# Nine runs of four modulation blocks instead of eighteen runs of two, between the weight products of a fused two-layer kernel

## The reference: what is computed

```python
mod = jax.nn.silu(c) @ w_mod[l] + b_mod[l]
sh_m, sc_m, ga_m, sh_f, sc_f, ga_f = [m[:, None, :] for m in jnp.split(mod, N_MOD, axis=-1)]
mod_c = jax.nn.silu(c_ctx) @ w_mod[l] + b_mod[l]
```

## Time and profile before

| what | value |
|---|---|
| median of 3 runs | 2073.24 us (2072.97 to 2073.39) |
| the profiled execution, own time | 2074.61 us |
| its span, first to last instruction | 2072.8 us |
| TensorE busy | 2036.8 us, 98% of the span |
| weight loads of TensorE busy | 1775.6 us, 86% |
| VectorE busy | 1526.2 us, 74% |
| ScalarE busy | 1036.0 us, 50% |
| moved by DMA | 454.53 MB, mean 219 GB/s |
| mean granted clock of TensorE | 0.996 |

### The profile page before, as it was taken

How to read it: one execution, slowest core, us unless ns; L and a number is a source line. 1 busy time by engine, 2 the same in 40 slices (tenths; PEclk the granted TensorE clock), 3 DMA queues, 4 the chain that set the end, 5 groups by cost and what they waited for, 6 DMA issues and landing times.

```text
span 2072.8 us, 29839 instructions
## 1 busy us (share of the span) xinstructions
PE 2036.8 (98%) x11900; PEld 1775.6 (86%) x11900; DVE 1526.2 (74%) x2369; ACT 1036.0 (50%) x1548; POOL 56.7 (3%) x57
## 2 busy tenths in 40 slices
PE   8999999999999999999999999999999999999998
PEld 8999999878888888898888888878888888888886
DVE  6888886869798786678888896576766756645655
ACT  6876445656423323545555555555445434434543
POOL 0000010110000000000000000200000000000000
PEclk9999999999999999999999999999999999999999
DMA  7778898667534586444447987555875765565553
GB/s 284 241 255 298 299 340 270 240 198 256 167 101 153 207 297 236 149 136 143 132 143 275 374 300 260 182 165 180 292 263 187 254 212 191 190 213 190 191 192 113
DMA packets 124251, 454.53 MB, mean 219 GB/s; under 512 B 14288, under 2 KB 14672, under 8 KB 123472
## 3 DMA queue, kind: packets, MB, share of 16 engines
q1 hardware_dynamic: 124112, 452.62, 64.4%
HBM read 448.35 MB, written 4.22 MB: 218 GB/s over the span
## 4 chain that ended last, share of the span: by engine, by line
PE 72%; DVE 2%; ACT 1%; issue 0%; DVEq 0%; ACTq 0%
PE bank L923 72%; DVE WL L1643 1%; DVE AR L1650 0%; DVE AR L1643 0%; DVE SR L1650 0%; ACT WH L1228 0%; ACT AR L1228 0%; ACT AR L1229 0%; ACT L1229 0%; PE bank L1080 0%; PE bank L1119 0%; ACT SR L1229 0%; DVE WF L1681 0%; DVE AR L1738 0%; DVE AR L2142 0%
## 5 line engine op out<-in xcount | busy, mean ns | idle before, releaser
L923 PE MATMUL bank<-SR,WH 128*128 128x512 f32 (+1 forms) x5216 | 1395.3, 354 | 16.8 <-DVE WL L1643 7.9
L1643 DVE TENSOR_TENSOR WL<-WF,WH 128x1024 fp32r<-128x1024 f32 x636 | 775.7, 1226 | 266.1 <-ACT WH L1228 262.6
L1228 ACT ACTIVATE WH<-WF 128x1024 fp32r<-128x1024 f32 x636 | 671.5, 1057 | 539.7 <-PE bank L923 472.1
L923 PE MATMUL bank<-SR,WL 128*128 128x256 f32 (+1 forms) x3936 | 924.2, 287 | 1.7 <-DVE SR L1650 1.7
L923 PEld LDWEIGHTS bank<-SR,WH 128*128 128x128 f32 x5216 | 832.2, 190 | 65.9 <-issue 20.5
L923 PEld LDWEIGHTS bank<-SR,WL 128*128 128x128 f32 x3936 | 744.9, 189 | 123.3 <-DVE SR L1650 3.3
L923 PE MATMUL bank<-WH,SR 128*128 128x512 f32 x1280 | 395.0, 389 | 0.0
L923 PEld LDWEIGHTS bank<-WH,SR 128*128 128x128 f32 x1280 | 240.3, 188 | 49.5
L1228 ACT ACTIVATE AR<-bank 128x256 f32<-128x256 f32 (+1 forms) x261 | 110.1, 426 | 291.7 <-PE bank L923 288.0
L923 PE MATMUL bank<-WL,SR 128*128 128x512 f32 x640 | 249.0, 389 | 0.0
L1643 DVE TENSOR_TENSOR AR<-AR 128x256 f32<-128x256 f32 (+3 forms) x374 | 158.3, 455 | 51.8 <-ACT AR L1229 34.8
(11 more groups left out here) (98 smaller groups left out, 563.5 us busy)
## 6 DMA issues: line engine op xcount, KB each, us to landing
WF<-in_mlp SPq DMA_DIRECT2D x256, 512.0 KB, 3.7
WF<-in_mod SPq DMA_DIRECT2D x192, 512.0 KB, 5.3
WF<-in_w_in SPq DMA_DIRECT2D x176, 512.0 KB, 4.5
WF<-in_a_in SPq DMA_DIRECT2D x64, 512.0 KB, 5.4
WF<-in_a_out SPq DMA_DIRECT2D x32, 512.0 KB, 6.4
WF<-in_ple_g SPq DMA_DIRECT2D x32, 512.0 KB, 4.8
WF<-in_w_out SPq DMA_DIRECT2D x32, 512.0 KB, 5.0
WF<-in_pw SPq DMA_DIRECT2D x16, 512.0 KB, 3.7
```

The source lines that it names most:

```text
L923: return tensor.matmul(o, l, r, start=start, stop=stop, skip_group_check=True)
L1228: return scalar.activation(o, x, f, scale=scale)
L1643: return vector.tensor_tensor(o, a, b, op)
```

## The change

`add_spread` puts four "p" blocks into the ring where it put two, and is called half as often. The 36 blocks are the same, their order among themselves is the same, and all other blocks keep their order. In each pair of runs that becomes one, it is the first run that moves back to the place of the second. The runs that stood before (behind `xb` tiles 7, 9, 11, 13, 15; `gate` 1, 3, ..., 15; `aout` 0, 3, 6, 9, 12) become runs behind `xb` 9 and 13, `gate` 1, 5, 9, 13 and `aout` 0, 6, 12.

```diff
     def add_spread():
-        for _ in range(2):
+        for _ in range(4):
             if spread:
...
             add("xb", "a_in", 2 * j + n)
-            if j > 2 and n:
+            if j in (4, 6) and n:
                 add_spread()
...
         if j == 1:
             add("gates", "a_gates", 3)
-        if j % 2:
+        if j % 4 == 1:
             add_spread()
         add_mod(int(j % 2 or j == 14), 64)
     for j in range(16):
         add("aout", "a_out", j)
-        if j % 3 == 0:
+        if j % 6 == 0:
             add_spread()
```

## The result

| kernel | median, us | runs | ratio to before, same chip |
|---|---|---|---|
| before | 2074.31 (2071.26 to 2077.58) | 19 | |
| after | 2079.38 (2076.07 to 2083.29) | 19 | 1.0022 [1.0016, 1.0029] |
| after, a second time on another occasion | 2079.03 (2077.14 to 2080.57) | 11 | 1.0023 [1.0014, 1.0032] |

The change makes the kernel slower by 0.22 to 0.23%, some 4.7 us. The measured median, 2079.38 us, lies 1.2 us above the upper end of the forecast range (2078.2); as a ratio on the 2073.24 us of the prediction it is 2077.8, at that end. The forecast was +1.8 us (ratio 1.0009) and "no change". The profiled execution after took 2081.52 us, its span is 2079.7 and its mean granted clock 0.991 (before 2074.61, 2072.8 and 0.996). It is 2.1 us longer than the median of its kernel, whose mean granted clock over the 19 runs is 0.994, so it shows more half clock than a usual execution.

A forecast was written before the change was run, and what follows sets the result against it. TensorE, busy 98% of the span, was taken as the bound. Summed: -2.9 (nine merges) + 0.3 (`gates` 3 saving lost) + 3.2 (`gates` 3 wait) + 1.2 (`aout` 3) = +1.8 us, median 2073.24 to 2075.0; range 2071.0 to 2078.2.

The forecast's parts named there:

- no change: Whole kernel: a median within the 0.2% bound, 2069.1 to 2077.4 us, given 82%.
- +1.2 us for `aout` 3: At `aout` 3 to 4: the run taken out turns into 1.18 us longer TensorE wait for VectorE's vector.
- the clock: Rival: the 3.2 us pause at `gates` 3 halves TensorE's clock, 1.7 us on top, 2076.7; chance 18%.
- the price of a merge: TensorE, each merge: two runs of two at 1.18 become one of four at 2.04, saving 0.32 us; nine save 2.9.
- the chain of waits at `gates` 3: Second `gate` 2 load late, so ScalarE's high part and sigmoids late, PSUM banks full, second `gates` 3 block waits: 3.2 us.
- the rival of another price for the run of four: A run of four costs more or less than 2.04 us; each 0.1 us worth 0.9 in all; no chance given.
- The wait at `gates` 3: TensorE ahead of the second `gates` 3 block: start at about 154.0 instead of 150.82, 3.2 us.
- lower bound: At `gates` 3: wait of 1.6 us if the second `gate` 2 load takes 3.7 us and lands at 150.9.
- VectorE does not run ahead: Before `gates` 3: VectorE has hardly a pause from 134 to 147.2, so the low part freeing the slot ends at 147.20.
- comes later, at full price: The run of four behind `aout` 6 costs its 2.04 us, leaving 0.32 - 1.18 = -0.86 of this merge.
- The ring too short in more places: Rival: late loads behind runs at `gate` 5, 9, 13; two places at 3.2 us each give 2081.4; chance 10%.
- the `gates` 3 saving lost: At `gates` 3: this merge's 0.32 us is not realised, as TensorE's fourth tile waits for VectorE until 150.00.

The follow-up runs named there:

- `aout` back: The changed kernel with runs of two again behind `aout` 3 and `aout` 6, eight merges kept: 2074.72 us, ratio 1.0003 to before.
- `aout` moved: The changed kernel with only the run of four behind `aout` 6 placed behind `aout` 3 instead: 2075.36 us, ratio 1.0000 to before.
- again: The changed kernel itself, unaltered, timed and profiled once more: 2079.03 us, ratio 1.0023 to before.
- filled: The changed kernel plus unused constant matmuls, ten ahead of the second `gates` 3 block, fourteen ahead of the first `aout` 4 block: 2076.30 us, ratio 1.0014 to before.
- `gates` 3 back: The changed kernel with runs of two again behind `xb` 15 and `gate` 1, eight merges kept: 2075.86 us, ratio 1.0005 to before.
- `gates` 3 moved: The changed kernel with only the run of four at `gates` 3 placed ahead of its pair of blocks: 2076.16 us, ratio 1.0003 to before.
- both back: The changed kernel with the merges at `gates` 3 and at `aout` 3 and 6 both undone, seven kept: 2072.68 us, ratio 0.9992 to before.
- seven merges: The changed kernel with the `gates` 3 run ahead of its pair and runs of two kept behind `aout` 3 and 6: 2072.47 us, ratio 0.9987 to before.
- only `gates` 3: The kernel before with one merge only, the runs behind `xb` 15 and `gate` 1 merged behind the `gates` 3 pair: 2074.80 us, ratio 1.0004.

## Why the prediction was wrong

The sum had +1.2 us for `aout` 3 and nothing for the run of four behind `aout` 6 beyond its 2.04, nor for the clock, which stood as a rival only. Those two missing terms are the step that failed; the price of a merge and the chain of waits at `gates` 3 held, with the wait there sized too large.

**The price of a merge: right.** Where nothing waits, a first run taken away gives 1.18 us and the longer run costs 0.86: `aout` 2 to 3 goes from +1.11 to -0.06 in the table. From `gate` 2 to the last `gate` tile, where three merges are whole and one run moves out, TensorE gains 2.11 us (from +2.36 to +0.25), against 3 x 0.32 + 1.18 = 2.14. The run itself takes 1.92 to 1.93 us, so the rival of another price for the run of four is out where its blocks are in time.

**The wait at `gates` 3: right mechanism, too large a term.** The chain load, ScalarE's high part, full banks, TensorE is as foretold. The term was 3.2 us with a lower bound of 1.6. The second block lost 1.61 against the first in the first profile and 1.04 in the second, and 1.13, 1.24 and 1.32 with `aout` back, `aout` moved and this merge alone: the lower bound and below. Two parts were off. The slot came free at 145.52 and not at 147.20. I had written that VectorE does not run ahead because the first run is gone. It did: the run starts 1.67 us earlier (141.40, before 143.07), VectorE's low part 1.68, and the 0.86 by which the run is longer comes only behind that, so TensorE's own lead at the block is 0.80. And the load took 4.5 us (3.9 us in the second profile), between the 3.7 and 5.3 of the earlier trace rows.

**The clock: the rival that I held for a third as likely as the wait.** Half clock stood behind this wait in four of the five profiled executions that had it unfilled (after, again, `aout` back, `aout` moved; not in the one with only this merge). It costs 1.55 us: `gate` 2 goes from +0.81 to +2.36. The pauses that brought it here were 1.74 to 2.33 us, shorter than the 3.2 for which I gave it that chance. I had drawn that chance from one execution, in which the pause near 1350 us brought no half clock. In nine of the fourteen profiled executions the same pause did. The Trainium skill ("TensorE: Matmul & The Clock Gate", Part 1: The HAM clock gate) says that half rate follows an idle stretch. The filled kernel agrees with it (clock 0.9958 against 0.9939), the waits of 2.02 and 2.99 us without half clock behind them show that here it is not so each time.

**`aout` 3: the step that failed most.** I forecast -0.86, made of 0.32 saved and 1.18 that only turn into a wait. That much is there: `aout` 4 starts 3.7 us after VectorE gets the vector (266.03 to 269.72 before, 268.82 to 272.52 after, 267.74 to 271.44 again), whatever TensorE did before. Three things were missing.
- The prediction said of the four-block run only that it "comes later, at full price". It comes at more. While VectorE waits for the vector, SyncE issues no load for 7.4 to 9.1 us (after, again, `gates` 3 back), and the run now needs four blocks right behind that gap. With the clock up it cost 1.3 (filled), 1.9 (again) and 2.2 us (`gates` 3 back) on top. I had looked at the ring behind the runs, and not at the loads of a run itself.
- The wait that grew by 1.18 was followed by half clock in three of five unfilled executions. The two hide one another, so that together they cost 1.3 to 2.6 us (`aout` 4 to 6 in the table, less 0.86; 1.6 with `gates` 3 moved).
- The vector's own time. VectorE stood 4.95 us in the one profile of before, but 6.54, 6.37, 6.08 and 5.43 us in four kernels with the runs of two at `aout` unchanged (`aout` back, both back, seven merges, only `gates` 3). The 2.85 us by which the wait grew in the first profile are 1.18 by the run and 1.7 by this scatter, which kernels without the merge show too.

**The ring too short in more places: wrong places, right kind.** No wait came at `gate` 5, 9 and 13. The late blocks were those of a run, at `aout` 6.

**The sum again.** Nine merges with the `gates` 3 saving lost, -2.6; the wait there +1.3 and its clock some +1.2 (1.55 in four of five); the run missing at `aout` 3 +1.2; late blocks or half clock at `aout` +1.9 on average of six profiles. That is +3.0 of the measured 4.7 (interval 3.3 to 6.0). The rest isn't placed. The mean clock fell by 0.0019 of 2074 us, 3.9 us lost to the clock at most, and the two places explain about 3 of these. Stretches such as the one at 459.3 come in both profiles of the change, but also in four of the other kernels, two of them faster than before, and not in the one of before. Single profiles can't say whether the change makes them more frequent.

**Uncertainty.** The range ended at +0.24%. It holds the ratio on the 2073.24 us that it was made for, but not the measured median; that the ratio still falls inside, with 3 us of the cost in terms that the sum did not have, is no merit of the sum. The chance of 82% for "no change" was too high. I had set the lower clock and late blocks apart as rivals of which one comes true; both did.

## What to carry to other kernels

Before a burst of work is made longer, check whether its own loads can be there: look for the last gap in the load queue ahead of it and count how many slots come free between the gap and the burst. A run of two that stands inside another engine's wait is free here, so leave it there and merge elsewhere; a run of four at the same place is free only in part. The same nine runs, two of them moved, gave 0.9984 instead of 1.0022, and seven merges with the runs of two left at `aout` gave 0.9987. A pause of about 2 us of TensorE has to be counted twice, once as time and once as the risk of half clock, and a wait read from one profile may be off by more than the effect.

## What the runs showed of the hardware

- At the two places TensorE's granted clock fell to 0.50 for 3.4 us or twice that behind pauses of 1.74, 1.83, 1.95, 2.21, 2.33, 2.37, 3.59 and 3.62 us, but in other executions did not behind pauses of 1.68, 1.87, 1.90, 1.95, 2.02 and 2.99 us. The length of the pause does not decide alone. With matmuls in the pauses it did not fall.
- The same holds where the change moves nothing. In the fourteen profiled executions a pause of 1.92 to 1.96 us near 530 us was followed by half clock in ten, one of 1.93 near 1340 in nine, one of 3.05 near 1350 in nine, and those of 1.67 near 360 and 1.70 near 950 in none.
- The matmuls of one block (32 weight columns, two column groups) take 1.05 us alone and 1.07 us with the other two groups at work beside them, so two blocks that arrive apart cost nearly double.
- VectorE's wait for a vector of 512 KB varied from 4.88 to 6.64 us between executions; both ends come from kernels in which `aout` is ordered alike. What sets it was not tried.
